# A hybrid decoder layer with mixture of experts: the last two experts' rows summed by TensorE without warming matmuls, and the final tiles shared by three engines

## What is computed

```python
def rmsnorm(x, g):
    xf = x.astype(jnp.float32)
    y = xf * lax.rsqrt(jnp.mean(xf * xf, axis=-1, keepdims=True) + RMS_EPS)
    return (y * g.astype(jnp.float32)).astype(x.dtype)
...
    for e in range(N_EXPERTS):          # 16 experts, each row uses 2
        ye = (jax.nn.silu(hf @ w_gate[e]) * (hf @ w_up[e])) @ w_down[e]
        out = out + combine[:, e:e + 1] * ye.astype(jnp.float32)
...
    x = x + gt2 * moe(hf, w_router, b_router, w_gate, w_up, w_down)
    return x, h_last, new_lru_buf, new_conf_buf
...
    y_prompt = rmsnorm(xp, g_final)
    y_sample = rmsnorm(xs, g_final)
```

## Time and profile before

| | |
|---|---|
| median of 3 runs | 936.18 us |
| lowest and highest | 932.68, 939.60 us |
| the profiled execution: time | 937.74 us |
| its span (first to last instruction) | 935.9 us |
| mean granted TensorE clock | 0.973 of 2.4 GHz |
| busy: PE, DVE, ACT, POOL | 866.3, 675.2, 426.9, 304.2 us |

### The profile page before, as it was taken

The page is one execution under the profiler, slowest core; times in us unless marked ns, Lnnn a source line. Parts: engine busy times, 40 slices in busy tenths (PEclk is TensorE's granted clock), DMA queues, the critical chain, the costliest instruction groups (busy, mean ns, idle before and its releaser), DMA issues.

```text
span 935.9 us, 13274 instructions
## 1 busy us (share of the span) xinstructions
PE 866.3 (93%) x5477; PEld 727.8 (78%) x5477; DVE 675.2 (72%) x922; ACT 426.9 (46%) x391; POOL 304.2 (33%) x177
## 2 busy tenths in 40 slices
PE   3899999989999999999999987899999999999983
PEld 3798888989988888899984556788877878777761
DVE  2429999999795693733024477788889988988748
ACT  5443232323246526151201213577777767777623
POOL 5344555736520230253311141122232543331110
PEclk9999999999999999999999997899999999999987
DMA  9978677412120140342446123789999999999932
GB/s 315 340 233 282 234 239 275 144 48 91 46 90 2 46 136 1 101 140 91 163 169 238 46 107 143 254 284 349 348 375 336 356 343 370 363 342 338 327 111 96
DMA packets 76538, 194.41 MB, mean 208 GB/s; under 512 B 7972, under 2 KB 49060, under 8 KB 66093
## 3 DMA queue, kind: packets, MB, share of 16 engines
q1 hardware_dynamic: 71245, 182.19, 55.1%
q0 software_dynamic: 5088, 10.99, 4.4%
q10 hardware_dynamic: 144, 0.38, 0.1%
HBM read 185.41 MB, written 16.47 MB: 216 GB/s over the span
## 4 chain that ended last, share of the span: by engine, by line
PE 37%; DVE 34%; DMA 15%; ACT 5%; issue 4%; POOL 2%; SPq 2%; POOLq 0%; DVEq 0%; ACTq 0%
PE ps L1287 19%; DVE ps L1689 13%; DVE slot_c L1848 8%; DMA ring_a<-in_w_up 6%; PE ps L1375 6%; PE ps L1275 5%; DMA ring_a<-in_w_gate 4%; DVE slot_a L1848 3%; POOL w_lo L758 2%; ACT slot_c L1083 2%; PE ps L1469 2%; SPq L540 2%; PE ps L1319 1%; DMA region_b<-in_w_ada 1%; DVE region_b L1984 1%
## 5 line engine op out<-in xcount | busy, mean ns | idle before, releaser
L758 POOL TENSOR_TENSOR w_lo<-ring_a,w_hi 128x2048 fp32r<-128x2048 f32 x28 | 136.8, 4889 | 242.9 <-ACT w_hi L943 242.9
L1848 DVE TENSOR_TENSOR slot_c<-ring_a,slot_c 128x2048 fp32r<-128x2048 f32 x72 | 163.9, 2287 | 24.3 <-ACT slot_c L1083 24.1
L1287 PE MATMUL ps<-hm_hi,w_hi 128*128 128x272 f32 x720 | 151.8, 292 | 8.1 <-ACT region_c L982 4.0
L1083 ACT ACTIVATE slot_c<-ring_a 128x2048 fp32r<-128x2048 f32 x72 | 137.3, 1916 | 46.0 <-DMA ring_a<-in_w_gate 24.9
L1287 PE MATMUL ps<-hm_hi,w_lo 128*128 128x272 f32 x720 | 148.6, 289 | 0.0
L1287 PE MATMUL ps<-hm_lo,w_hi 128*128 128x272 f32 x720 | 148.4, 288 | 0.0
L1689 DVE SCALAR_TENSOR_TENSOR ps<-region_b,rt,ps 128x512 f32<-128x512 f32 x208 | 137.6, 745 | 0.0
L1287 PEld LDWEIGHTS ps<-hm_hi,w_hi 128*128 128x128 f32 x720 | 112.7, 189 | 23.7 <-issue 18.7
L1469 PE MATMUL ps<-slot_c,xgt_hi 128*128 128x512 f32 x384 | 126.7, 400 | 2.2 <-DVE slot_c L1848 1.1
L1287 PEld LDWEIGHTS ps<-hm_lo,w_hi 128*128 128x128 f32 x720 | 113.2, 189 | 0.0
L1287 PEld LDWEIGHTS ps<-hm_hi,w_lo 128*128 128x128 f32 x720 | 112.8, 190 | 0.0
(11 more groups left out here) (334 smaller groups left out, 1423.8 us busy)
## 6 DMA issues: line engine op xcount, KB each, us to landing
ring_a<-in_w_gate SPq DMA_DIRECT2D x32, 1024.0 KB, 8.4
ring_a<-in_w_up SPq DMA_DIRECT2D x32, 1024.0 KB, 8.5
ring_a<-in_w_down SPq DMA_DIRECT2D x32, 1024.0 KB, 7.4
ring_a<-in_w_in SPq DMA_DIRECT2D x24, 1024.0 KB, 7.1
region_c<-in_w_ada SPq DMA_DIRECT2D x20, 1024.0 KB, 6.0
ring_a<-in_w_conf_o SPq DMA_DIRECT2D x4, 1024.0 KB, 5.8
ring_a<-in_w_lru_o SPq DMA_DIRECT2D x4, 1024.0 KB, 5.3
region_d<-in_w_ada SPq DMA_DIRECT2D x3, 1024.0 KB, 13.0
```

Source lines behind the costliest of these rows:

```text
L758: g.tensor_tensor(w_lo[:, q % 2], raw[split_at[q] % 2], w_hi[:, q % 2].bitcast(F32), ALU.subtract)\
L1083: s_.activation(hi_slot(n), raw_slot(n), ACT.Copy).then_inc(unit_hi, 1)
L1287: ins = mm(ps[:, bank(n) + h, 0:HALF], w[:, q % 2, k, m * P:(m + 1) * P], x[:, k, h * HALF:(h + 1) * HALF], start=(k == 0 and w is w_hi an ...
L1848: v.tensor_tensor(lo_slot(n), raw_slot(n), hi_slot(n).bitcast(F32), ALU.subtract).then_inc(unit_lo, 1)
```

## The change

- Expert 14's rows are no longer scattered. They stay in SBUF as `row_hi[0]`, `row_lo[0]` with a one-hot matrix `hot[0]`; expert 15's are `[1]`. GpSimd's last scatter is expert 13's.
- The end of the experts is written out by hand. TensorE: `gate_up(15)`, half of `down(14)`, `h_turn(15)`, the other half, then `down(15)` into banks 0 and 1 from `xgt_hi`, `xgt_lo`, which hold expert 15's hidden rows now. VectorE: `hidden(15)` comes after one low part and no longer after three. ScalarE copies the hidden rows ahead of the last weight unit. Expert 15's rows are copied in two halves.
- SP reads the accumulated rows into buffers of their own (the three `xg` and two pieces of a weight buffer), tile 4 third, and no longer waits for all units' low parts.
- TensorE: the 24 matmuls of ones are gone; a tile is `sums_before(t)`, `add_rows(t, 0)`, `add_rows(t, 1)`: 2 identity and 8 one-hot matmuls, where it was 2 and 4. The tiles' banks are taken in another order.
- Final loop: VectorE's product with gt2 is written in place, in PSUM, and the addition reads it there. The last multiply of VectorE is replaced by a multiply by the gain on GpSimd and a scaling by the root's inverse on ScalarE (`scale_rows`), for tile t - 1 between the square and the root of tile t, for tiles 3 and 4 at the end. The small operands of the root lie in PSUM. ScalarE loads the root's table ahead of the loop.

The diff, cut to its core:

```diff
-        ya = carve(ring_a, 0, (NT, D))
+        ya = [region_d[:, D:2 * D], region_e[:, 0:D], ring_a[:, 2 * UNIT:2 * UNIT + D], ring_a[:, 2 * UNIT + D:3 * UNIT],
+              region_d[:, 0:D]]
         yo = carve(region_c, 7168, (NT, D))
         junk = carve(region_c, 2 * D, (D,))
-        row_hi, row_lo = slot_c[:, 1, 0, 0:D], slot_c[:, 1, 1, 0:D]
+        row_hi = [slot_c[:, 0, 0, 0:D], slot_c[:, 1, 0, 0:D]]
+        row_lo = [slot_c[:, 0, 0, D:2 * D], slot_c[:, 1, 1, 0:D]]
...
-            first = (0, 2, 5)[t % 3]
+            first = (2, 5, 0)[t % 3]
...
             sp.wait_ge(ov_done, 1)
-            for t in range(NT):
-                sp.dma_start(ya[0:TILES[t], t, :], acc_scr[t * P:t * P + TILES[t], :]).then_inc(rows_in[t], 16)
+            sp.wait_ge(xgt_ps, NE)
+            for t in (0, 1, 4, 2, 3):
+                if t == 2:
+                    sp.wait_ge(unit_lo, len(units) - 3)
+                sp.dma_start(ya[t][0:TILES[t], :], acc_scr[t * P:t * P + TILES[t], :]).then_inc(rows_in[t], 16)
...
+            pool.wait_ge(bc2_in, 16 * 4)
+            for t in range(NT):
+                n = TILES[t]
+                pool.wait_ge(fin_dve, t + 1)
+                g.tensor_tensor(yo[0:n, t, :], x1[0:n, t, :], gfin_bc[0:n, :], ALU.mult).then_inc(gain_ok, 1)
...
+            next_high()
+            silu(NE - 1)
+            next_high()
+            next_high()
+            act.wait_ge(ht_ps, NE)
+            s_.activation(xgt_hi[:, 0:GC, :], ps[:, 4, :].rearrange("p (k c) -> p k c", k=DE // P), ACT.Copy)\
+              .then_inc(ht_ok, 1)
+            next_high()
+            act.wait_ge(unit_used, len(units) - 2)
+            act.wait_ge(w_slot_ok, NE - 1)
+            s_.activation(row_hi[0].rearrange("p (h n) -> p h n", h=2), ps[:, 5:7, :], ACT.Copy,
+                          scale=w_slot[:, NE - 2:NE - 1]).then_inc(y_act, 1)
             act.wait_ge(unit_used, len(units))
             act.wait_ge(w_slot_ok, NE)
-            s_.activation(row_hi.rearrange("p (h n) -> p h n", h=2), ps[:, 5:7, :], ACT.Copy,
-                          scale=w_slot[:, NE - 1:NE]).then_inc(y_act, 1)
+            for h in range(2):
+                s_.activation(row_hi[1][:, h * 512:(h + 1) * 512], ps[:, h, :], ACT.Copy,
+                              scale=w_slot[:, NE - 1:NE]).then_inc(y_act, 1)
...
+            def scale_rows(t):
+                n = TILES[t]
+                act.wait_ge(gain_ok, t + 1)
+                act.wait_ge(fin_rstd, t + 1)
+                s_.activation(yo[0:n, t, :], yo[0:n, t, :], ACT.Copy, scale=rstd[0:n, t:t + 1]).then_inc(fin_ok, 1)
+            s_.activation(spt[:, 2, 0:1], eps_ln[:, :], ACT.Sqrt)
             for t in range(NT):
                 n = TILES[t]
                 act.wait_ge(fin_dve, t + 1)
                 if t:
                     act.wait_ge(fin_act, t)
                 s_.activation(junk[0:n, :], x1[0:n, t, :], ACT.Square, accum_out=ssq[0:n, t:t + 1]).then_inc(fin_act, 1)
+                if 0 < t < NT - 1:
+                    scale_rows(t - 1)
                 act.wait_ge(rms_ask, NT + t + 2)
-                s_.activation(nt1[0:n, t:t + 1], ssq[0:n, t:t + 1], ACT.Sqrt).then_inc(rms_sqrt, 1)
+                s_.activation(fin_q[0:n, t:t + 1], fin_w[0:n, t:t + 1], ACT.Sqrt).then_inc(rms_sqrt, 1)
+            for t in (NT - 2, NT - 1):
+                scale_rows(t)
...
+            def down_half(e, c, hi, lo, first):
+                n = unit_no[("down", e, c)]
+                pe.wait_ge(unit_lo, n + 1)
+                w_h = hi_slot(n).rearrange("p (k n) -> p k n", k=2)
+                w_l = lo_slot(n).rearrange("p (k n) -> p k n", k=2)
+                for k in range(2):
+                    for x, w in ((hi, w_h), (lo, w_h), (hi, w_l)):
+                        for h in range(2):
+                            ins = mm(ps[:, first + h, :], x[:, 2 * c + k, :], w[:, k, h * DE:(h + 1) * DE],
+                                     start=(c == 0 and k == 0 and x is hi and w is w_h),
+                                     stop=(c == 1 and k == 1 and w is w_l))
+                ins.then_inc(unit_used, 1)
             def down(e):
                 pe.wait_ge(ht_lo_ok, e + 1)
                 if e:
                     pe.wait_ge(y_act, e)
                 for c in range(2):
-                    n = unit_no[("down", e, c)]
-                    pe.wait_ge(unit_lo, n + 1)
-                    w_h = hi_slot(n).rearrange("p (k n) -> p k n", k=2)
-                    w_l = lo_slot(n).rearrange("p (k n) -> p k n", k=2)
-                    for k in range(2):
-                        for x, w in ((act_hi, w_h), (act_lo, w_h), (act_hi, w_l)):
-                            for h in range(2):
-                                ins = mm(ps[:, 5 + h, :], x[:, 2 * c + k, :], w[:, k, h * DE:(h + 1) * DE],
-                                         start=(c == 0 and k == 0 and x is act_hi and w is w_h),
-                                         stop=(c == 1 and k == 1 and w is w_l))
-                    ins.then_inc(unit_used, 1)
+                    down_half(e, c, act_hi, act_lo, 5)
...
+            def add_rows(t, i):
+                n, banks = TILES[t], sum_banks(t)[0]
+                pe.wait_ge(hot_ok, i + 1)
+                for h in range(2):
+                    pe.wait_ge(y_act, NE - 1 + i * (h + 1))
+                    mm(ps[0:n, banks[h], :], hot[i][:, t * P:t * P + n], row_hi[i][:, h * 512:(h + 1) * 512],
+                       start=False, stop=False)
+                    pe.wait_ge(row_lo_ok, 1 + i * (h + 1))
+                    ins = mm(ps[0:n, banks[h], :], hot[i][:, t * P:t * P + n], row_lo[i][:, h * 512:(h + 1) * 512],
+                             start=False, stop=(i == 1))
+                return ins
             xg_turn(0)
             keep_busy(1, 32)
-            for e in range(NE):
+            for e in range(NE - 1):
                 gate_up(e)
-                if e < NE - 1:
-                    xg_turn(e + 1)
+                xg_turn(e + 1)
                 if e + AHEAD < NE:
                     index(e + AHEAD, (e + AHEAD) % 2)
                 if e:
                     down(e - 1)
                 h_turn(e)
-            down(NE - 1)
+            gate_up(NE - 1)
+            pe.wait_ge(ht_lo_ok, NE - 1)
+            pe.wait_ge(y_act, NE - 2)
+            down_half(NE - 2, 0, act_hi, act_lo, 5)
+            h_turn(NE - 1)
+            down_half(NE - 2, 1, act_hi, act_lo, 5)
+            pe.wait_ge(ht_lo_ok, NE)
+            for c in range(2):
+                down_half(NE - 1, c, xgt_hi, xgt_lo, 0)
...
-            keep_busy(4, 24)
             for t in range(NT):
                 sums_before(t)
-                last_expert(t)
+                add_rows(t, 0)
+                add_rows(t, 1).then_inc(sum_ps, 1)
...
+            next_low()
+            hidden(NE - 1)
+            next_low()
+            next_low()
+            dve.wait_ge(ht_ok, NE)
+            v.tensor_tensor(xgt_lo[:, 0:GC, :], ps[:, 4, :].rearrange("p (k c) -> p k c", k=DE // P),
+                            xgt_hi[:, 0:GC, :].bitcast(F32), ALU.subtract).then_inc(ht_lo_ok, 1)
+            next_low()
+            dve.wait_ge(y_act, NE - 1)
+            v.scalar_tensor_tensor(row_lo[0].rearrange("p (h n) -> p h n", h=2), ps[:, 5:7, :], w_slot[:, NE - 2:NE - 1],
+                                   row_hi[0].bitcast(F32).rearrange("p (h n) -> p h n", h=2),
+                                   ALU.mult, ALU.subtract).then_inc(row_lo_ok, 1)
+            for h in range(2):
+                dve.wait_ge(y_act, NE + h)
+                v.scalar_tensor_tensor(row_lo[1][:, h * 512:(h + 1) * 512], ps[:, h, :], w_slot[:, NE - 1:NE],
+                                       row_hi[1].bitcast(F32)[:, h * 512:(h + 1) * 512],
+                                       ALU.mult, ALU.subtract).then_inc(row_lo_ok, 1)
...
-                    y1, xr = ya[0:n, t, :], x1[0:n, t, :]
+                    xr = x1[0:n, t, :].rearrange("p (h n) -> p h n", h=2)
                     dve.wait_ge(sum_ps, t + 1)
+                    ch.do(v.tensor_tensor(sum_banks(t)[1], sum_banks(t)[1],
+                                          gt2_bc[0:n, t // 4, :].rearrange("p (h n) -> p h n", h=2), ALU.mult))
                 if t:
                     n_ = TILES[t - 1]
-                    r_, q_, w_ = (x[0:n_, t - 1:t] for x in (rstd, nt1, ssq))
+                    r_, q_, w_ = (x[0:n_, t - 1:t] for x in (rstd, fin_q, fin_w))
                     dve.wait_ge(fin_act, t)
-                    v.tensor_scalar(w_, w_, 1.0 / D, RMS_EPS, ALU.mult, ALU.add).then_inc(rms_ask, 1)
+                    v.tensor_scalar(w_, ssq[0:n_, t - 1:t], 1.0 / D, RMS_EPS, ALU.mult, ALU.add).then_inc(rms_ask, 1)
                 if t < NT:
-                    ch.do(v.tensor_tensor(y1.rearrange("p (h n) -> p h n", h=2), sum_banks(t)[1],
-                                          gt2_bc[0:n, t // 4, :].rearrange("p (h n) -> p h n", h=2), ALU.mult))
```

(17 more changed lines are left out.)

61 lines of the change are left out of this document (24 added, 37 removed).

## The result

The changed kernel takes 926.4 us (median of 15 runs, 922.76 to 930.40) against 936.25 us (15 runs, 932.39 to 939.60) of the kernel before. The ratio is 0.9893, with a 95% interval of 0.9877 to 0.9909: 9.8 us, or 1.1%, less. The forecast was 927.0.

The account below looks back on a forecast made before the run. Bound: full DMA while experts run, then expert 14's scatter and row read, then VectorE's tiles. Start 6.4 us earlier, TensorE-bound tiles, last output at 924.4: 9.2 us off the median 936.18 gives 927.0 us; range 923.5 to 932.8.

Parts of the forecast that it names:

- Both parts of the start: Before the final loop: without expert 14's scatter and with down(15) earlier, VectorE starts at 903.5 instead of 909.94, 6.4 us.
- The clock: TensorE from expert 15's down product through the sums: 2.4 GHz throughout, as its idle stretch shrinks from 4.0 to 0.6 us.
- the place where it fails most easily: TensorE's idle stretch near 893.5, before down(15): put at 0.6 us; the prediction fails most easily if it is longer.
- The rival that the start moves less because of the clock: down(15) at half clock as long as before: start 2.6 to 3 us later, time 929.8; chance 0.15.
- the slower case: Clock falls near 893.5 and stays at 1.2 GHz through down(15) and all sums: time 949; chance 0.04.
- The loop: Final loop's five tiles: TensorE's 3.58 us per tile becomes the bound, 3.8 for the last; VectorE's own work 3.2.
- The rival in which they block each other: Final loop: GpSimd's and VectorE's wide operations exclude each other, each tile takes 5.4 us, time 934; chance 0.08.
- Edits priced at nothing: Second hot table, earlier root-table load, new sequence of halves and banks: no cost; the hot table, if uncovered, 0.6 us.

Follow-up runs that it names:

- experiment 4: The changed kernel with expert 15's hidden rows and transposes back in their old order, still without expert 14's scatter; ratio to the kernel before 0.9933.
- experiment 5: The changed kernel with expert 14's rows scattered to memory and read back as before; ratio to the kernel before 0.9984.
- experiment 6: The changed kernel with expert 14's scatter kept and 120 small matmuls in TensorE's idle stretch before the sums; ratio to the kernel before 0.9940.
- experiment 10: The changed kernel run once more, unaltered; median 926.57 us, ratio to the kernel before 0.9885.
- experiment 2: The kernel before with only its final loop changed (gain on GpSimd, scaling on ScalarE, product kept in PSUM); ratio to the kernel before 0.9943.
- experiment 1: The changed kernel with the 24 warming matmuls put back between the down product and the sums; ratio to the kernel before 0.9902.
- experiment 8: The changed kernel with GpSimd finishing tile 0's memory part in advance, not waiting for VectorE's last low part; ratio to the kernel before 0.9900.
- experiment 3: The changed kernel with the old final loop put back; ratio to the kernel before 0.9926.

## Why the prediction was right

Counted from the start of the last weight copy (891.56 in the forecast, 889.25 in the profile after), the steps stand so:

| step | forecast, us | measured, us |
|---|---|---|
| down product of expert 15 starts | 2.39 | 2.40 |
| first identity matmul | 8.04 | 8.13 |
| VectorE's first multiply | 11.94 | 11.90 |
| VectorE's fifth multiply | 26.54 | 26.43 |
| ScalarE's last square | 29.14 | 28.93 |
| ScalarE's last root | 30.54 | 30.30 |
| last output issued | 32.84 | 32.63 |
| end of the span | 35.14 | 35.15 |

That the last row agrees to 0.01 is chance: single steps are off by up to 0.24 and cancel. VectorE got the first tile 0.13 sooner after the first identity matmul than forecast, and the end came 2.52 us after the last output's issue, not 2.30. So is part of the agreement in whole times (927.0 forecast, 926.4 measured), since the forecast started from the median of three runs that spread over 7 us.

**Both parts of the start, together.** The forecast had 6.4 us there; it was 6.48 (18.38 to 11.90). Experiments 4 to 6 show that neither half has it alone. Without the scatter, but in the old order, the start moves 2.13 us (18.38 to 16.25); in the new order, but with the scatter, 0.23 at most (18.15). Before, two paths of nearly the same end led to the first sum: the scatter with the row read, which landed at 906.94, and the down product at half clock with the warming matmuls behind it, which ended at 906.59. Who shortens one finds the other.

**The clock.** Forecast: 2.4 GHz throughout, given an idle stretch of 0.6 us. It was 0.95, by the bracket at 891.65, and 1.59 in the changed kernel's second execution (experiment 10). The clock stood at 1.00 all the same. The step's size was wrong and its conclusion held; the forecast had called this the place where it fails most easily, and named no row that shows how long a wait the clock bears. The rival that the start moves less because of the clock, and the slower case with it, didn't occur in the change, but their mechanism is real: experiment 4 has it at 1.54 us, experiment 5 at 2.42. The forecast put 2.6 to 3 on it for the down product. The kernel before did lose 2.60: its 24 matmuls took 8.33 us (896.75 to 905.08), and 5.73 in the changed kernel (891.65 to 897.38). In experiments 2 and 4, in the same old order, they took 7.26 and 7.27, some 1.5 more, since the clock was back sooner: by 897 in experiment 4 (0.73 in 896 to 898), between 902 and 903 before. What such a fall costs thus differs from one execution to the next. At half clock a matmul took 0.43 us (898.63 to 900.33 for four, before), somewhat less than the twice 0.234 of the forecast. No run here took the slower case to its end, with all sums at half clock.

**The warming matmuls.** Leaving them out is worth the 1.33 us of experiment 1, and it is safe only since nothing idle precedes the sums: in experiment 6, 120 of the same kind bring the clock's 2.42 us back.

**The loop.** Forecast 3.58 per tile on TensorE and 3.8 for the last, measured 3.57, 3.58, 3.58 and 3.80. VectorE's own period was put at 3.2 and is 3.25 (experiment 2): three of its four small operations take 0.22 or 0.23, and the next starts 0.26 later. It still waits 0.23 us per tile for TensorE (the brackets at 908.30 and 911.88), where 3.58 less 3.2 would leave 0.38. This cost nothing, and shows how near the second bound lies. ScalarE's scaling was put at 1.06 and takes 1.13. At the end three engines finish side by side: tile 4's gain on GpSimd ends at 920.56, VectorE's root step at 920.61 and ScalarE's scaling of tile 3 near 920.7, so a shorter step on one of them alone would give about 0.1 us at most. The parts of the change don't add up: 4.8 for the loop alone and 6.48 for the start would be 11.3, and are 9.19, as TensorE's four more matmuls per tile make it the bound.

**GpSimd and VectorE.** The rival in which they block each other, 934 us, had 0.08 and didn't occur: VectorE's 1.23 beside GpSimd's 2.37. By the Trainium skill, "SBUF — State Buffer", section "SBUF: two separate sides", such a lock goes to whichever operation starts first, and of VectorE's operations it concerns only those with two SBUF inputs or in a two-port mode. The trace agrees with both halves: one input from PSUM meets no block in the final loop, and in experiment 8, where VectorE's operation with two SBUF inputs had started 0.66 us earlier, a wait for its end (1.62 us) and then GpSimd's own 2.4 would make 4.0, and 3.88 was measured.

**Edits priced at nothing.** The early hidden(15), the row reads beside the last weights, the second table and the root's earlier table load cost nothing that shows: the first identity matmul has no wait for rows, and the tail adds up without them. ScalarE's extra copy held up the last weight copy in experiments 3, 6 and 8, but that copy isn't on the path: in experiment 3 VectorE's first multiply comes 14.40 us after the copy before the last, and 14.39 in the changed kernel. What they may do ahead of the last copy is not separated from the scatter of whole executions, of which it is smaller.

**The rest.** The tails give 9.19 us, the medians 9.84. The difference of 0.65 is within the interval of the ratio (8.5 to 11.5 us), and no run here assigns it.

## What to carry to other kernels

When two paths end at nearly the same time, price a change to one of them by the end of the other, and try each half alone: here one half gave 2.1 us, the other nothing, and both together 6.5. Count from an event that the change can't move: single executions can then be compared to a tenth of a microsecond although whole times scatter by 3. The start of the last weight copy did this only to 0.4 us, as the change had put another copy ahead of it; the weight copy before that did it to 0.1. And before warming matmuls are put in or taken out, look at what TensorE does just ahead of them: 24 of them cost 1.3 us behind steady work, and 120 were worth 2.4 in an idle stretch.

## What the runs showed of the hardware

- In experiment 8 GpSimd's 128x1024 multiply beside VectorE's subtraction with two SBUF inputs took 3.88 us instead of 2.40, and VectorE's took its usual 2.28. GpSimd's started second. I had expected VectorE to be the one that loses.
- Four identity matmuls that took 1.72 us of the chain at a granted clock of 1.00 took 3.78 after 7.6 us without a matmul, at 0.50. Idle stretches of 0.95 us and, in experiment 10, 1.59 us between matmuls left the clock at 1.00; with waits of 1.11 and 2.15 us around four transposes it stood at 0.50 afterwards (experiment 4).
- Of VectorE's operations of one column in the changed kernel, three take 0.22 to 0.23 us and follow one another in 0.26 (907.33, 907.59, 907.85), while two others take 0.15 and 0.16 (905.87, 907.13). PSUM is not what divides them, since the two have an operand there as well. The three take a factor per row from memory (`rstd`, or `w_`, the mean square), the two only constants or none; and a one-column operation of the experts' part that reads one with no operand in PSUM (L2045, 16 times) takes 0.21. No run changes this alone.
